# Attention heads q and k turned before they are stored, by block transposes, instead of by TensorE before they are used

## What is computed

```
proj = h @ w_in                                  # [1024, 8192], split into q, k, v, g of 2048 columns
q = rms_norm(q.reshape(S, 16, 128), q_g)         # 16 heads of 128; the mean square is over a head
k = rms_norm(k.reshape(S, 16, 128), k_g)
for each chunk j of 64 rows:                     # its band: 8 chunks to the left and itself
    s = q_j @ k_band^T * 128**-0.5 + bias
    p = softmax(where(valid, s, -1e30))
    o_j = p @ v_band
o = o * silu(g);  out = o @ w_out
```

## Time and profile before

| | |
|---|---|
| median of three executions | 2449.5 us |
| the profiled execution | 2450.25 us |
| its span, first to last instruction | 2448.4 us (so 1.85 us lie around it) |
| TensorE matmul busy | 2419.0 us, 99% of the span |
| VectorE / ScalarE / GpSimd busy | 64% / 45% / 50% |
| granted TensorE clock | 0.999 of full |
| transfers | 241196 packets, 329.21 MB, 134 GB/s mean |

### The profile page before, as it was taken

The page is one execution under the profiler, slowest core; times in us unless marked ns, Lnnn a source line. Parts: engine busy times, 40 slices in busy tenths (PEclk is TensorE's granted clock), DMA queues, the critical chain, the costliest instruction groups (busy, mean ns, idle before and its releaser), DMA issues.

```text
span 2448.4 us, 36045 instructions
## 1 busy us (share of the span) xinstructions
PE 2419.0 (99%) x13808; PEld 2076.6 (85%) x13808; DVE 1578.4 (64%) x2151; ACT 1105.7 (45%) x2052; POOL 1235.7 (50%) x883
## 2 busy tenths in 40 slices
PE   7999999999999999999999999999999999999999
PEld 6888898875588898899888899999988888788887
DVE  6965657588543386653766766666434489788863
ACT  5322223344544353322322226777534434888861
POOL 1645545430044455545555555555454445866664
PEclk9999999999999999999999999999999999999999
DMA  7554544493034345543332257454144343300034
GB/s 277 157 190 154 180 163 158 142 325 137 27 112 156 104 150 181 176 142 107 122 116 98 89 166 226 124 156 121 50 135 158 105 161 123 103 1 1 2 127 156
DMA packets 241196, 329.21 MB, mean 134 GB/s; under 512 B 19401, under 2 KB 173825, under 8 KB 239233
## 3 DMA queue, kind: packets, MB, share of 16 engines
q1 hardware_dynamic: 239552, 326.80, 40.3%
q10 hardware_dynamic: 1472, 0.10, 0.0%
HBM read 247.53 MB, written 79.33 MB: 133 GB/s over the span
## 4 chain that ended last, share of the span: by engine, by line
PE 91%; DVE 5%; issue 2%; ACT 1%; POOL 1%; DMA 1%; SPq 0%; DVEq 0%; ACTq 0%
PE ps L1182 23%; PE ps L1184 23%; PE ps L1183 23%; PE ps L1534 4%; PE ps L1707 2%; PE ps L1522 2%; PE ps L1688 2%; PE ps L1451 2%; PE ps L1470 2%; PE ps L1464 1%; DVE s_raw L2349 1%; PE ps L1375 1%; PE ps L1202 1%; PE ps L1434 1%; PE ps L1407 1%
## 5 line engine op out<-in xcount | busy, mean ns | idle before, releaser
L1068 POOL TENSOR_TENSOR w_lo<-raw,w_hi 128x512 fp32r<-128x512 f32 (+1 forms) x452 | 652.9, 1453 | 794.4 <-ACT w_hi L1813 758.8
L1813 ACT ACTIVATE w_hi<-raw 128x512 fp32r<-128x512 f32 (+1 forms) x456 | 282.9, 629 | 795.1 <-PE ps L1184 633.4
L1182 PE MATMUL ps<-w_hi,s_hi 128*128 128x256 f32 (+2 forms) x832 | 262.8, 316 | 0.8 <-POOL w_lo L1068 0.3
L1183 PE MATMUL ps<-w_lo,s_hi 128*128 128x256 f32 (+2 forms) x832 | 262.0, 315 | 0.0
L1184 PE MATMUL ps<-w_hi,s_lo 128*128 128x256 f32 (+2 forms) x832 | 262.0, 315 | 0.0
L1068 POOL TENSOR_TENSOR w_lo<-raw_wide,w_hi 128x512 fp32r<-128x512 f32 x112 | 174.0, 1560 | 131.3 <-ACT w_hi L1813 131.3
L2462 DVE TENSOR_TENSOR u<-u,ps 128x1024 f32<-128x1024 f32 (+1 forms) x96 | 116.4, 1212 | 148.9 <-PE ps L1184 145.5
L1182 PE MATMUL ps<-w_hi,a_hi 128*128 128x256 f32 (+2 forms) x624 | 196.7, 315 | 0.0
L1183 PE MATMUL ps<-w_lo,a_hi 128*128 128x256 f32 (+2 forms) x624 | 196.6, 315 | 0.0
L1184 PE MATMUL ps<-w_hi,a_lo 128*128 128x256 f32 (+2 forms) x624 | 196.5, 315 | 0.0
L1182 PE MATMUL ps<-s_hi,w_hi 128*128 128x512 f32 x480 | 188.6, 393 | 3.2 <-DVE s_lo L2336 2.3
(11 more groups left out here) (341 smaller groups left out, 6214.6 us busy)
## 6 DMA issues: line engine op xcount, KB each, us to landing
raw<-in_w SPq DMA_DIRECT2D x159, 512.0 KB, 4.3
ada_c<-in_ada SPq DMA_DIRECT2D x14, 2304.0 KB, 10.8
blk<-u SPq DMA_DIRECT2D x54, 512.0 KB, 4.0
raw_wide<-in_w SPq DMA_DIRECT2D x32, 512.0 KB, 4.6
blk<-c SPq DMA_DIRECT2D x27, 512.0 KB, 3.4
blk<-m1s SPq DMA_DIRECT2D x27, 512.0 KB, 3.3
ada_first<-in_ada SPq DMA_DIRECT2D x12, 768.0 KB, 16.0
r_g<-blk SPq DMA_DIRECT2D x8, 1024.0 KB, 9.4
```

The source lines that it names most:

```text
L1068: pool.tensor_tensor(w_ring(w_lo, n), w_source(n), w_ring(w_hi, n).bitcast(F32), ALU.subtract)\
L1182: pe.matmul(out, a_hi_, b_hi_, start=first, stop=False, skip_group_check=True)
L1183: pe.matmul(out, a_hi_, b_lo_, start=False, stop=False, skip_group_check=True)
L1813: act.activation(w_ring(w_hi, n), w_source(n), ACT.Copy).then_inc(w_rounded, 1)
```

## The change

The quadrants of q and k are kept in the buffer in an order in which a VectorE transpose of 32 x 32 blocks turns them. The norm's multiplication goes to ScalarE, eight small activations a quadrant, placed between its weight roundings; VectorE keeps the reciprocals and gets one block transpose a quadrant. The stores of a turned quadrant are four transfers instead of one. The heads are then loaded with head dimension on the partitions: k in one transfer of 4 KB rows (its blocks are put in order when it is rounded), q in eight transfers whose runs are 128 B. TensorE turns no head any more. q and k are loaded for head h+2 instead of h+3, into two buffers instead of four; v and gates as before.

```
 # quadrant order in SBUF, wide blocks
-  return buf[:, :].rearrange("p (b n) -> p b n", b=4)
+  return buf[:, :].rearrange("p (j b i) -> p j b i", b=4, i=32)
 # SyncE: store
+  if kind == "unit":
+      for g in range(4):
+          at = 512 * a + P * g
+          sp.dma_start(turned_rows(s)[256*c:256*c+256, at:at+P].rearrange("(j i) t -> i j t", i=32),
+                       quad_buf(s, quad)[32*g:32*g+32, :].rearrange("i (j t) -> i j t", t=P)).then_inc(stored[quad], 16)
+      return
 # SyncE: wide_block
   if s - 1 in UNIT:
+      wide_store(s - 2, "c22")
       wide_store(s - 2, "c21")
       wide_store(s - 2, "c12")
...
   sp.wait_ge(w_split, product_end(s, 2))
   if following:
       wide_load(R21, s + 2)
+      wide_store(s, "c11")
   else:
+      wide_store(s, "c11")
       load_raw(R11, s + 2); load_raw(R12, s + 2)
       sp.wait_ge(stored["c11"], stored_count(s + 2)); load_raw(R21, s + 2)
-  wide_store(s, "c22")
+  if not following:
+      wide_store(s, "c22")
...
 # SyncE: the loads of a head
+  def a_load_qk(h):
+      n, c = h % 2, slice((h % 4) * P, (h % 4) * P + P)
+      if h > 1: sp.wait_ge(a_hlow, 4 * (h - 1))
+      for s, dst in ((AQ[h // 4], a_q), (AK[h // 4], a_k)):
+          in_memory(s)
+          if dst is a_k:
+              sp.dma_start(dst[n] ..., turned_rows(s)[c, :]).then_inc(aqk_in[n], 16)
+              continue
+          for m in range(8):
+              a, g = divmod(m, 4)
+              sp.dma_start(dst[n][:, 4*a:4*a+4, 32*g:32*g+32],
+                           turned_rows(s)[c, m*P:m*P+P].rearrange("d (b t) -> d b t", t=32)).then_inc(aqk_in[n], 16)
...
   for h in range(1, AH):
+      if h + 1 < AH: a_load_qk(h + 1)
       if h + 1 < AH: sp.wait_ge(a_max, NT * h); a_load_bias(h + 1)
       if h == 1:
-          a_load(3)
+          a_load_v(3)
...
       sp.wait_ge(a_odone, NT * h)
       if h + 3 < AH:
-          a_load(h + 3)
+          a_load_v(h + 3)
           for a in range(2): a_load_g(h + 3, a)
 # TensorE: a_turn_head and its calls are gone (head 0 in block 27, the others in the loop)
 # ScalarE
+  def unit_scale(s, quad):
+      q, e, whole = QUADS.index(quad), s - wide_of(s), quad_buf(s, quad)
+      act.wait_ge(u_sums, inverse_count(s, quad))
+      heads = whole[:, :].rearrange("p (h f b i) -> p b h f i", h=2, f=4, b=4)
+      for m in range(8):
+          part = heads[:, m // 2, m % 2]
+          ins = act.activation(part, part, ACT.Identity, scale=u_st[e][:, 1, q, m:m + 1])
+      ins.then_inc(u_scaled, 1)
 # where: c21 of the pair before, ahead of the next block's first rounding; c12 of the pair before, behind
 # m1s_copy in product 1; c11 and c22 between the first two roundings of products 4 and 6.
 # In block 27: c21 at i == 0 ahead of product_slots(27, 1); c12 at i == 1, behind m1s_copy(27) and post,
 # ahead of product_slots(27, 3).
+  def a_head_high(h, n):
+      if n == 0: act.wait_ge(aqk_in[h % 2], 144 * (h // 2 + 1))
+      if (h, n) == (1, 0):
+          for quad in QUADS: act.wait_ge(stored[quad], stored_count(28))
+      if h > 1 and n == 0: act.wait_ge(a_sdone, NT * (h - 1))
+      ...  # k: Copy into the order of the rows; q: Identity with the gain; both from SBUF
 # VectorE, wide_block: unit_scale goes; in its place
+  def unit_inverse(s, quad):    # two reciprocals of 8 columns, once the roots are there
+  def unit_turn(s, quad):
+      flat = quad_buf(s, quad)[:, :]
+      dve.wait_ge(u_scaled, unit_count(s, quad))
+      dve.transpose(flat, flat).then_inc(p_unit, 1)
 # its order for c22 of the last pair: evict c21, unit_inverse c22, unit_sums c21 (two), unit_turn c22 (two).
 # In block 27: evict c12, four weight sums, unit_turn c21 (two), unit_sums c12 (two), evict(27, "c11"),
 # unit_inverse c12, unit_turn c12 (two), evict(27, "u2").
 # VectorE, a_head_low: both inputs now from SBUF (q raw and q high, k raw and k high), no PSUM
```

More of the change, by code:

```diff
@@ L170, in rows_of, with turned_rows, stored_count @@
             return blk[s][0:(512 if BLOCKS[s][1] == "F" else S) * width].rearrange("(t n) -> t n", n=width)
+        def turned_rows(s):
+            return blk[s][0:512 * S].rearrange("(n t) -> n t", t=S)
+        def stored_count(blocks):
+            return 16 * (blocks + 3 * sum(1 for u in UNIT if u < blocks))
         ident = sb("ident", [P, P])
@@ L1295, in block_product @@
                         if (s, i, k) == (27, 6, 3):
+                            pe.wait_ge(ev, evicted(27, "c21"))
                             a_scores(0)
@@ L1365, in next_half @@
                 return between
-            def a_turn_head(h, n):
-                if n == 0:
-                    pe.wait_ge(ah_in[h % 4], 48 * (h // 4 + 1))
-                if h:
-                    pe.wait_ge(a_hlow, 1 if (h, n) == (1, 0) else 4 * h + n)
-                for m in range(4):
-                    tr = pe.transpose(ps[:, a_piece_bank(h, n), m * P:(m + 1) * P],
-                                      a_half((a_q[h % 4], a_k[h % 4]), n)[:, m], ident[:, :])
-                tr.then_inc(a_hturned, 1)
             def a_scores(e):
@@ L1901, in wide_block @@
                 for p, i in enumerate(WIDE_ORDER):
+                    ahead, before = PRODUCT[s, i] + RING, s - 1 in UNIT
+                    if p == 0 and before:
+                        for e in range(2):
+                            unit_scale(s + e - 2, "c21")
                     if p == 1:
@@ L1904, in wide_block @@
                             m1s_copy(s + e)
-                    ahead = PRODUCT[s, i] + RING
+                        for e in range(2 if before else 0):
+                            unit_scale(s + e - 2, "c12")
                     hi(ahead)
+                    if p in (4, 6):
+                        for e in range(2):
+                            unit_scale(s + e, "c11" if p == 4 else "c22")
                     hi(ahead + 1)
-                    quad = {0: "c12", 3: "c11", 5: "c22", 6: "c21"}.get(p)
-                    if quad and (p or s - 1 in UNIT):
+                    if p == 6:
                         for e in range(2):
-                            post(s + e if p else s + e - 2, quad)
+                            post(s + e, "c21")
                     if p < 6 or s + 2 in WIDE:
@@ L1914, in wide_block @@
                         hi(ahead + 3)
+                    if p == 0 and before:
+                        for e in range(2):
+                            post(s + e - 2, "c12")
+                    if p in (3, 5):
+                        for e in range(2):
+                            post(s + e, "c11" if p == 3 else "c22")
             def first_block(l):
@@ L1954, in projections @@
                     for i in range(7 if wide_of(s) is None else 0):
+                        if i == 0 and s - 1 in UNIT:
+                            for e in range(2):
+                                unit_scale(s + e - 2, "c21")
                         if i < 6:
@@ L2427, in wide_block @@
                     unit_sums(s + e, "c11")
-                for e in range(2):
-                    unit_scale(s + e, "c11")
                 wide_evict(s, "u3")
+                unit_inverse(s, "c11")
                 if s + 2 in WIDE:
@@ L2434, in wide_block @@
                 for e in range(2):
+                    unit_turn(s + e, "c11")
+                for e in range(2):
                     unit_sums(s + e, "c22")
-                for e in range(2):
-                    unit_scale(s + e, "c22")
                 wide_evict(s, "c21")
+                unit_inverse(s, "c22")
                 for e in range(2):
@@ L2441, in wide_block @@
                 for e in range(2):
-                    unit_scale(s + e, "c21")
+                    unit_turn(s + e, "c22")
+                unit_inverse(s, "c21")
             def evict(s, what):
```

183 lines of the change are left out of this document (109 added, 74 removed).

## The result

The changed kernel takes 2457.71 us (median of 7 runs, 2455.38 to 2459.37), the kernel before 2450.23 us beside it (7 runs, 2449.23 to 2450.76): 1.0031 of the time, 95% interval 1.0021 to 1.0041. It is slower by 7.5 us; 2443.4 was forecast, with 2433 to 2457 as the range. The profiled execution of the changed kernel took 2455.38 us (span 2453.6), 5.1 us more than that of the kernel before, and its trace accounts for these 5.1 us. The other 2.3 us lie between the median and this execution, the fastest of the seven, so they stand in no trace of the changed kernel.

A forecast was written before the change was run, and what follows sets the result against it. TensorE was taken to bound the q and k projection and attention. From 2450.25 us, - 28.2 + 16.1 + 1.5 + 1.5 + 1 + 1 + 1 = - 6.1 gave 2444.15, as median 2443.4 us, range 2433 to 2457.

The forecast's parts named there:

- Removed, - 28.2: Attention: 64 TensorE turnings of half heads at 0.44 us go, 28.2 us less; a head takes 15.4 us.
- Pairs, + 1.5: q and k projection, pairs 21, 23, 25: ScalarE's scales delay a rounding and low part, 0.5 us each, 1.5 in all.
- Into block 27, + 16.1: Block 27: R22's landing, c21's stores and c12's scales in series delay product 3 from 1456.5 to 1472.6, 16.1 us.
- The clock, + 0: TensorE's clock behind the wait before block 27's product 3: the prediction had no term for it.
- Scores wait for low parts, + 1: Start of attention, head 0: VectorE's four low parts end 1 us after TensorE arrives, 1 us given back.
- Attention, + 3.5: Attention: 1.5 us for head 1's rounding awaiting block 27's stores, 1 for first heads' loads, 1 for VectorE's two-operand low parts.
- rival D: Attention: VectorE's low parts and GpSimd delay each other at the shared port, 12 us instead of 1; 2454.5 us, chance 0.12.
- Loading ahead in the steady state, just in time: Attention: q and k of head h+2 land 10.7 us after issue, against 10.9 until ScalarE needs them.
- Rival C: Attention: q's 128 B runs cost as much as 512 B ones, 1.5 us for each of 13 heads; 2463 us, chance 0.08.
- rival B: Step into block 27 mostly hidden as R22 and c21's stores pass other transfers, 2.7 us remaining; 2430 us, chance 0.12.
- E: Doesn't pay, 2447 to 2452 us: half-speed block transposes add 2.3 us to three pairs and block 27 each; chance 0.16.

The follow-up runs named there:

- one_turn: Kernel before the change with one TensorE transpose instead of four in each of 64 half-head turnings (values wrong, time only): 2430.27 us, 0.9919.
- q_one_transfer: Changed kernel with a head's q loaded like k in one transfer of 4 KB rows, its low part in four VectorE instructions: 2456.06 us, 1.0022.
- r22_first: Changed kernel with SyncE issuing R22 of block 27 ahead of the first head's and bias loads: 2449.95 us, 1.0002.
- busy_fill: Changed kernel with spare matmuls in TensorE's waits in block 27, 80 before product 2 and 45 before product 3: 2457.01 us, 1.0027.
- busy_fill2: Changed kernel with spare matmuls in TensorE's waits in block 27, 82 before product 2 and 72 before product 3: 2456.23 us, 1.0024.
- lows_spread: Changed kernel with GpSimd's four output weight low parts in attention steps 14, 22, 30 and 38 instead of 14 to 17: 2455.79 us, 1.0022.
- o_split_moved: Changed kernel with VectorE's low parts of the attention output one step later: 2455.56 us, 1.0022.
- o_split_halves: Changed kernel with VectorE's attention output low part in two halves, ending steps 4 and 6 instead of whole ending step 3: 2455.48 us, 1.0023.
- four edits of order: Changed kernel, block 27: R22 and c21's stores before head loads, c21 turned after first weight sum, c12 scaled after product 3's roundings: 2440.10 us, 0.9957.
- head1_late: Kernel with the four edits of order, plus ScalarE's first rounding of head 1 and its low part one step later: 2440.78 us, 0.9961.
- best: head1_late plus GpSimd's output weight low parts spread, VectorE's output low parts halved, head 2's q and k issued before block 27's store wait: 2433.19 us, 0.9929.

## Why the prediction was wrong

The step that failed most is the attention stage. The prediction priced what the added work costs there at 3.5 us, and 10.4 us were lost: it had no term for GpSimd's four weight low parts and VectorE's output low parts, old work that no longer fits in a head of 15.4 us. The second is the step into block 27, where R22 landed 18.3 us after the first store and not 12.8. The third is TensorE's clock behind the wait, which it had at nothing.

Its steps one by one, in the trace's own terms (the profiled executions, 2450.25 and 2455.38 us). The sum was - 6.1, the measured net + 5.1. Of the 14.3 us between the forecast and the median these 11.2 are in the trace, 2.3 lie between the median and the profiled execution, and 0.75 is the forecast's own step from one execution to the median, which seven executions of the kernel before (2450.23) do not bear out.

- **Removed, - 28.2**: right. 26.8 by one_turn, or 26.4 by the intervals; the steady head takes 15.4 us as predicted.
- **Pairs, + 1.5**: right. c12 of the last pair is evicted at 1440.55 instead of 1439.21, 1.3 us.
- **Into block 27, + 16.1**: right in mechanism, too small. Product 3 was to be 17.6 us late with the pairs' share and was 20.8. The term of the sum that was mis-sized is R22's landing. It priced 3.7 MB at the 292 GB/s of the earlier trace rows, 12.8 us from the first store at 1438.5; they took 18.3, until 1456.8. The rows of the stretch, first the changed kernel, then q_one_transfer:

```profile
1440.00:1450.00 10.00, 9.66 (x79) 9.41 (x79) 3.49 (x3) 5.55 (x18) 2.53 (x2) 1.00 0.89 193
```

```profile
1440.00:1450.00 10.00, 9.66 (x74) 9.20 (x73) 4.53 (x6) 5.84 (x18) 3.44 (x3) 1.00 0.91 244
```

 The queue was nearly full at 193 GB/s. With q in long runs R22 is issued at 1446.7, five us sooner counted from the first store, and still lands at 1455.9, 16.1 us behind that store: what stands ahead on the queue sets the landing, by its bytes and packets, and not the moment of issue. (r22_first, which takes the head loads from in front of it, has its second weight sum at 1448.8.) Of the 5.5 us missed, q's short runs are 2.2. What the other 3.3 are was not tried (the stores of turned quadrants are the new kind of transfer left in it). Product 3 is late by only 3.2 us more than said, since the prediction rounded R22's landing up to 1452 and counted the pairs' 1.5 us beside it. Behind the landing the chain was right in size: 20.4 us to product 3, 20.6 in the prediction (which let c21's eight stores be issued by 1460, where its own 0.46 us each give 1460.7).
- **The clock, + 0**: a missing step. 1.8 us behind product 3, at a granted 0.50 until 1481. The prediction had a wait of 9 us before that product and no price for TensorE's speed after it.
- **Scores wait for low parts, + 1**: 0.56, at 1501.77, behind the first tile's first matmul and so within the first interval. Up to that tile only 0.4 us was added besides (21.7 us from product 3 at full clock, against 23.06 - 1.76 = 21.3). The first tile is 20.8 + 1.8 + 0.4 - 1.76 = 21.2 us late; 16.8 was predicted. That is 4.4 us of the miss.
- **Attention, + 3.5** (1.5 stores, 1 load, 1 low parts) **over fifteen intervals**: measured 26.4 - 16.0 = 10.4, which is 6.9 us of the miss. By interval, against 12.98 for the first (14.74 - 1.76) and 15.4 for the rest: the first + 2.4 (the 0.56 us above, and TensorE's wait of 1.2 us behind ScalarE's wait for the stores, which is 1.8 us where 1.5 was predicted), the second + 2.0 (head 2's load, where 1 us was priced), the third + 2.2 (GpSimd's four low parts: missing from the prediction), five of + 0.7 each, 3.5 in all (VectorE's output low part ahead of a low part of q: likely rival D in five heads, where I had spread 1 us over all), and 0.3 in small pieces.
- **Loading ahead in the steady state, just in time**: right. ScalarE waits for a_k in 11 heads, by 2.8 us for head 2 and 0.9 at most for the others, and none of it but head 2's reaches TensorE. **Rival C** is out, since it wants up to 3 us in each head; **rival B** too, since products 2 and 3 waited 10.3 and 6.3 us. **Rival D** was likely right on its ground and was wrong on its extent; that its 2454.5 lies near the result is luck. **E** said that it does not pay, and it does not, but for other reasons: E named block transposes at half speed, and they take 1.20 to 1.25 us for 128x1024, as other operations of that size do.

So two kinds of error. The steps that the prediction worked out were within a few us, and the one large cost among them came out too small. And what it left out was other engines' work in that loop: it asked what the new operations cost and not which old ones, hidden in 17.15 us, no longer fit in 15.4. GpSimd's 14.5 us in one head and VectorE's output low part of 1.39 us in five were to be seen in the trace of the kernel before.

The 2.3 us by which the median lies above the profiled execution are probably the clock again, in the second interval. In five kernels that leave this stretch as it is (busy_fill, busy_fill2, lows_spread, o_split_moved, o_split_halves) that interval is 19.3 to 19.7 us in the profiled execution, in the changed kernel and r22_first 17.4. The stretch behind TensorE's wait for head 2, in the changed kernel, then in lows_spread:

```profile
1525.00:1529.00 4.00, 4.00 (x33) 3.96 (x34) 3.54 (x13) 3.21 (x10) 3.74 (x4) 1.00 0.90 196
```

```profile
1525.00:1529.00 4.00, 3.96 (x19) 3.86 (x20) 2.86 (x11) 2.04 (x6) 3.47 (x3) 0.57 0.30 39
```

In all five TensorE waited 1.7 to 2.1 us there, and behind it the granted clock fell to about half for some 4 us; in the changed kernel and r22_first it waited 1.5 and 1.4 us and the clock stayed full. A clock of 0.57 over 4 us is 1.7 us lost. So head 2's late load can cost twice, and the profiled execution escaped the second part. That the other six executions did not is an inference, for they have no trace.

## What to carry to other kernels

When a loop's bound engine gets shorter, list every engine's work and longest run of work in each iteration against the new period, the iterations with extra work first. When a value takes another path to memory, look at the one queue on which its stores, the next stage's loads and an urgent operand stand in written order: here four edits of order were worth 17.6 us. A wait removed at one place is only a gain if the next load behind it is early too (head1_late alone: nothing; with head 2's load earlier: 3.4 us in the first two intervals, of which head 3's load took 2.4 back in the trace). When such a wait is long, look at the granted clock of the stretch behind it.

## What the runs showed of the hardware

- Behind a wait of 6.3 us TensorE ran at 1.2 GHz (granted 0.50) for its first 4 us of work, which cost 1.8 us; spare matmuls in the wait kept it at 2.4 GHz. With 3.3 us of that wait left unfilled the clock still fell (0.85 and 0.81 over the stretches 1475 to 1480 and 1480 to 1485).
- In attention, where TensorE also has shorter pauses, the same fall followed last waits of 1.7 to 2.1 us in five kernels (0.57 over 4 us in lows_spread, so 1.7 us lost), and did not follow one of 1.85 us in best: the length of the last wait alone does not tell.
- A packet of 128 B costs some 10 ns (7 to 11) more on the queue than its bytes in long runs, as a mean over all loads of q (667 us over 65280 packets).
- A VectorE block transpose (32 x 32) of 128x1024 float32 takes 1.20 to 1.25 us, as its other operations of that size do (1.22 for an eviction).
- ScalarE's eight activations on 128 columns with a scale start 0.30 us apart, 2.45 us for eight, as the prediction estimated from the wide ones.
